# A ninth weight unit beside the ring, a first gather that also turns, a later weight vector, and the last expert's sums kept in the banks

## The chip, the cores and the metric

The kernel runs on one core of one Trainium2 chip. The time is that of the device in microseconds (us), from the program's start to its end; the median of several executions counts. All engines work side by side: TensorE (PE) multiplies, VectorE (DVE) and ScalarE (ACT) do elementwise work, GpSimd (POOL) helps a little, and SyncE (SP) issues nearly all transfers (DMA).

## What is computed

One layer of a decoder on 336 token rows (272 of a prompt with its 16 meta tokens, 64 of samples): a mixing part (RWKV-7 heads and a convolution), then a mixture of 32 experts of which each token takes 4, then a last RMS norm. The change touches the expert part and the last norm. Cut to those, the reference is:

```python
h2 = rms_norm(x, norm_ffn)
logits = h2 @ w_router + b_router
top_val, top_idx = lax.top_k(logits, TOP_K)          # 4 of 32
gates = jax.nn.softmax(top_val, axis=-1)
# for every expert e, on the tokens that chose it:
gt = jnp.minimum(xe @ w_gate[e] + b_gate[e], SWIGLU_LIMIT)
up = jnp.clip(xe @ w_up[e] + b_up[e], -SWIGLU_LIMIT, SWIGLU_LIMIT)
ye = ((up + 1.0) * gt * jax.nn.sigmoid(SWIGLU_ALPHA * gt)) @ w_down[e] + b_down[e]
x = x + (sum over the token's experts of gates * ye)
y = rms_norm(x, norm_final)
```

All weights are float32, 1024 x 1024 each: 12.6 MB per expert, 402.7 MB for the 32 experts.

## The kernel before

**Stages.** The first 245 us hold the mixing part. Then the router scores all tokens, and the loop over the 32 experts runs, four experts to a turn: expert 0 to 3 are written out ahead of the loop, 28 to 31 behind it. Each expert works on one block of 64 token slots.

**One expert on PE** (`body`). `gate_up` multiplies the block xT with w_gate (bank 0) and w_up (bank 1), eight chunks of 128 rows each, and adds the bias with two small bf16 products. Then `combine` of the expert before: six products that spread its rows ys back to the tokens, into six banks (`CMB_BANKS = [5, 4, 3, 2, 6, 7]`). Then `next_rows` gathers the next expert's rows from h by a one-hot matrix Pm (bank 5), `turn_act` transposes the activation, `turn_p` transposes the combining matrix, `turn` transposes the gathered rows, and `down` multiplies with w_down (bank 2). DVE clamps and multiplies (`glu`), adds the six banks to the running sum acc (`add_rows`), and makes the one-hot matrices and xT (`take_x`); ACT computes the sigmoid and copies banks out (`take_rows`, `take_act`, `take_down`).

**Weight units.** A weight matrix comes in two units of 2 MB (128 partitions x 16 KB), so an expert has six: k = 0 and 1 gate, 2 and 3 up, 4 and 5 down, 6 is the next expert's first, and so on. They lie in a ring of NSLOT = 8 slots, unit k in slot k % 8. PE counts `unit_used` up by one when it is through with a unit. SP issues the units in order, all in one queue: the first eight once their places are free of the stages before (`FREED_BY`), and unit k from 8 on when `unit_used` says that unit k - 8 has been used, in the code's words `UPRE + k - NSLOT + 1`, which is k - 7 uses in the expert part. PE waits for a unit's own semaphore (`landed`). The last unit of all comes in two halves.

**Ahead of expert 0** (lines 1828 to 1845 and the code ahead of the bodies). When `p_ready` says that DVE has made the one-hot matrix Pm0, PE gathers the block's rows from acc (L1834, 12 matmul records, bank 5), ACT copies them to xg (L1631), PE transposes them (L1841, bank 5), DVE multiplies by the norm weights into xT (`take_x(1)`, L2064), and the first gate product begins (L1856). Between them stand `idle_product`s, products of nothing that is used (L1813). A record here is one matmul instruction as the trace has it; a float32 product takes two of them.

**Rows h.** ACT writes h, the scaled rows for the gathers of experts 1 to 31, over words 0 to 3071 of the arena, which x2T, the turned input, held before.

**Behind expert 31.** `combine` of the last expert (L1910); `add_tile` on DVE adds the six banks to acc (L2199); ACT squares and sums each tile's rows (`norm`, L1685) and takes the root (`root`, L1691); DVE takes the reciprocal (L2204) and multiplies rows, reciprocal and gfin, the final norm's weights (L2205); SP stores the outputs. There are three tiles of tokens: 128, 128 and 80 rows. gfin, 512 KB (one row laid out over 128 partitions), is fetched by SP right ahead of the first weight unit (L1502).

## Time and profile before

| | us |
|---|---|
| median of 3 runs | 1222.55 |
| lowest and highest | 1222.38, 1223.22 |
| the profiled execution, whole | 1223.54 |
| its span, from the first instruction to the last | 1221.6 |

| engine | busy, share of the span |
|---|---|
| PE matmul | 97% |
| PE weight load | 44% |
| DVE | 37% |
| ACT | 16% |
| POOL | 3% |
| transfers, mean of 16 DMA engines | 85% |

A page of the profile has a line per engine over 40 equal slices of the span (30.5 us each), a digit for the busy tenths, and the bytes moved per slice. Below that one can ask for the chain of work that ended last, for the instructions in order of time, and for the busy time of each engine in stretches of one's own choice. PE's busy time is that of pipelined matmuls whose ends overlap the next one's start, so several records in a row are read as (end of the last - start of the first - length of one) / (number - 1), which is called the pitch below.

### The profile page before, as it was taken

What the parts mean: (1) busy time and instruction counts of PE and PEld (TensorE: products, weight loads), DVE (VectorE), ACT (ScalarE), POOL (GpSimd) and SP (SyncE); (2) the same over time, 40 slices, a digit from 0 to 9 for tenths busy, and PEclk for the clock granted to TensorE, in tenths of its full rate; (3) what the DMA queues carried; (4) which work ended last, traced back from release to release, by engine and by line L of the source; (5) the groups of instructions that cost most, each with busy time, mean ns of one, the idle gap of its engine ahead of it and who ended that gap; (6) DMA issues with size and microseconds to landing.
All of it is one profiled execution on the core that took longest, in us unless ns stands there. A gap on an engine that the chain in (4) does not pass through costs nothing.

```text
span 1221.6 us, 19136 instructions
## 1 busy us (share of the span) xinstructions
PE 1187.9 (97%) x8044; PEld 535.9 (44%) x8044; DVE 453.2 (37%) x993; ACT 199.4 (16%) x437; POOL 30.8 (3%) x34
## 2 busy tenths in 40 slices
PE   8999999999999999999999999999999999999995
PEld 6676799764333333333333333333333333333332
DVE  6899442253533322222322333322222222222224
ACT  3345323123101000100100001100010000001002
POOL 0000050030000000000000000000000000000000
PEclk9999999999999999999999999999999999999998
DMA  9524000398999999999999999999999999999994
GB/s 261 178 69 184 11 4 13 90 383 329 429 425 424 428 426 428 428 429 428 428 429 428 427 429 429 428 428 429 428 429 428 427 428 429 428 429 428 427 428 155
DMA packets 53596, 430.25 MB, mean 352 GB/s; under 512 B 12175, under 2 KB 25919, under 8 KB 28702
## 3 DMA queue, kind: packets, MB, share of 16 engines
q1 hardware_dynamic: 53314, 428.91, 85.1%
q8 instruction: 43, 0.70, 0.2%
q10 hardware_dynamic: 228, 0.55, 0.1%
q14 instruction: 11, 0.09, 0.0%
HBM read 424.92 MB, written 4.48 MB: 352 GB/s over the span
## 4 chain that ended last, share of the span: by engine, by line
PE 66%; DMA 19%; DVE 1%; ACT 1%; issue 0%; POOL 0%; DVEq 0%
PE bank L1856 41%; DMA ring<-in_w_up_dram 19%; PE bank L1834 6%; PE bank L1910 5%; PE bank L1096 3%; PE bank L1841 2%; PE bank L1181 2%; PE bank L1785 2%; PE bank L1461 1%; PE bank L1864 1%; PE bank L1051 1%; PE bank L1077 1%; PE bank L1882 1%; PE bank L1234 0%; PE bank L1230 0%; PE bank L1139 0%
## 5 line engine op out<-in xcount | busy, mean ns | idle before, releaser
L1856 PE MATMUL bank<-ring,arena 128*64 128x512 f32 x1536 | 342.2, 594 | 7.5 <-DMA ring<-in_w_up_dram 6.8
L1856 PE MATMUL bank<-arena 128*64 128x512 f32 x1536 | 342.5, 593 | 6.1 <-DMA arena<-in_w_up_dram 6.0
L1856 PEld LDWEIGHTS bank<-ring,arena 128*64 128x64 f32 x1536 | 109.1, 137 | 218.9 <-issue 200.6
L1856 PEld LDWEIGHTS bank<-arena 128*64 128x64 f32 x1536 | 108.9, 136 | 216.9 <-issue 199.4
L2131 DVE TENSOR_SCALAR arena<-bank 128x512 f32<-128x512 f32 x32 | 22.1, 692 | 380.2 <-PE bank L1864 380.2
L2145 DVE TENSOR_TENSOR arena<-arena,bank 128x512 f32<-128x512 f32 x186 | 113.7, 679 | 1.6 <-PE bank L1910 1.6
L540 PE MATMUL bank<-arena,ring 128*128 128x336 f32 x352 | 102.8, 447 | 0.3 <-ACT arena L357 0.3
L1910 PE MATMUL bank<-arena 64*128 64x512 f32 (+1 forms) x384 | 91.1, 606 | 0.7 <-issue 0.7
L1834 PE MATMUL bank<-arena 128*64 128x512 f32 (+1 forms) x384 | 89.5, 600 | 0.1
L2135 DVE TENSOR_SCALAR arena<-bank 128x512 f32<-128x512 f32 x32 | 22.1, 692 | 176.4 <-PE bank L1864 176.4
L540 PEld LDWEIGHTS bank<-arena,ring 128*128 128x128 f32 x352 | 65.8, 189 | 33.9 <-issue 2.5
L1631 ACT COPY arena<-bank 128x512 f32<-128x512 f32 x32 | 18.8, 587 | 368.0 <-PE bank L1834 368.0
L762 DVE SCALAR_TENSOR_TENSOR arena<-ring,arena 128x336 f32<-128x336 f32 x120 | 58.5, 562 | 0.0
L1644 ACT ACTIVATE arena<-arena 128x512 f32<-128x512 f32 x32 | 20.2, 631 | 227.7 <-DVE arena L2131 227.7
L1910 PEld LDWEIGHTS bank<-arena 64*128 64x128 f32 (+1 forms) x384 | 31.9, 172 | 52.7 <-issue 52.7
L1654 ACT COPY arena<-bank 128x512 f32<-128x512 f32 x32 | 18.8, 586 | 221.5 <-PE bank L1856 221.5
L1834 PEld LDWEIGHTS bank<-arena 128*64 128x64 f32 (+1 forms) x384 | 24.9, 136 | 61.9 <-issue 56.1
L1841 PEld LDWEIGHTS bank<-arena 128*128 128x128 f32 x256 | 35.8, 210 | 26.8 <-DVE arena L2145 25.2
L2087 DVE TENSOR_SCALAR arena<-arena 128x128 f32<-128x128 f32 (+1 forms) x96 | 27.5, 342 | 49.9 <-PE bank L1882 49.7
L1841 PE MATMUL bank<-arena 128*128 128x128 f32 x256 | 45.8, 301 | 0.0
L2133 DVE TENSOR_TENSOR arena<-arena 128x512 f32<-128x512 f32 x32 | 22.2, 693 | 22.3 <-ACT arena L1644 22.3
L1864 PE MATMUL bank<-arena 96*64 96x512 bf16 x128 | 24.9, 381 | 0.0
(359 smaller groups left out, 784.6 us busy)
## 6 DMA issues: line engine op xcount, KB each, us to landing
ring<-in_w_gate_dram SPq DMA_DIRECT2D x32, 2048.0 KB, 24.5
arena<-in_w_up_dram SPq DMA_DIRECT2D x32, 2048.0 KB, 27.6
ring<-in_w_down_dram SPq DMA_DIRECT2D x32, 2048.0 KB, 31.0
arena<-in_w_gate_dram SPq DMA_DIRECT2D x32, 2048.0 KB, 26.3
ring<-in_w_up_dram SPq DMA_DIRECT2D x32, 2048.0 KB, 28.8
arena<-in_w_down_dram SPq DMA_DIRECT2D x31, 2048.0 KB, 30.7
ring<-in_w_in_dram SPq DMA_DIRECT2D x11, 1024.0 KB, 7.9
ring<-in_w_out_dram SPq DMA_DIRECT2D x4, 1024.0 KB, 8.1
```

What stands on the lines that cost most here:

```text
L540: mm = M.matmul(bank[:, n % 4, 0:NT], w[:, c, b * P:b * P + P], hT[:, c, :], start=(c == 0), stop=(c == KC - 1))
L762: V.scalar_tensor_tensor(dst, src, w, dst, ALU.mult, ALU.add).then_inc(R["conv_step"], 1)
L1096: mm = M.matmul(dst[64 * i:64 * i + n, q, j, 0:n], lhs[64 * i:64 * i + n, q, j, 0:n], rhs[64 * i:64 * i + n, q, j, 0:n], start=True, stop= ...
L1181: mm = M.matmul(bank1(b)[64 * i:64 * i + n_out, j, 0:n_free], lhs(i, j), rhs(i, j), start=(first and j == 0), stop=(last and j == NPAIR - 1))
L1785: mm = M.matmul(bank[:, (d + 1) % 4, 0:NT], out_rows(cc)[:, P * d:P * d + P], yT[:, cc, :], start=(cc == 0), stop=(cc == 3))
L1834: mm = M.matmul(bank[64 * hb:64 * hb + 64, 5, :], sel[0:m, i, :], rows[0:m, i, 512 * hb:512 * hb + 512], start=(i == 0), stop=(i == 2))
L1841: mm = M.transpose(bank[:, b, m * P:m * P + P], src.rearrange("t (p q) -> t q p", q=4)[:, m, :], ident)
L1856: mm = M.matmul(bank[64 * hb:64 * hb + 64, b, :], tokens(cc), w[:, c, 512 * hb:512 * hb + 512], start=(cc == 0), stop=(w3 == 2 and cc == K ...
L1864: mm = M.matmul(bank[64 * hb:64 * hb + 64, b, :], esel[0:3 * NE, :], bias2[0:3 * NE, w3, 512 * hb:512 * hb + 512], start=False, stop=True)
L1910: M.matmul(bank[0:m, bk, :], PgT[64 * hb:64 * hb + 64, i, 0:m], ys[64 * hb:64 * hb + 64, :], start=not biased, stop=True).then_inc(F["cmb_ ...
L2087: last = V.tensor_scalar(Pg[0:m, i], b2(slot_iota[0:m, :], 2), col(i, m), gates[0:m, i, bass.ds(e, 1)], ALU.is_equal, ALU.mult)
L2145: V.tensor_tensor(o, o, bank[0:m, CMB_BANKS[k], :], ALU.add).then_inc(F["cmb_read"], 1)
```

## The change

**Second unit outside the ring.** Unit 1 is no longer in the ring. It is fetched in two halves of 1 MB into `second`: words 29824 to 31871 and 0 to 2047 of the arena, which is free once x2T has been transposed for the last time (`acc_turned` 6). Units 0, 2, 3, ... 8 take the eight slots (`place(k, shift=1)`: unit k in slot (k - 1) % 8 from then on). Unit 9 goes in when unit 0 has been used; unit k from 10 on waits for k - 7 uses, as before. Since h overlies the second half, ACT writes h only when two units have been used.

**First gather turned at once.** Gather, copy, transposition and the three idle products ahead of expert 0 go. In their place PE makes xT in two banks: 24 products whose stationary operand is a strided part of acc (every fourth column, 128 of them) and whose moving operand is Pm0 with 64 columns. Bank 5 gets the first half (`x0_done`), bank 4 the second (`x_done`). DVE scales each half by itself. The first gate unit waits for the first half alone, the second for both.

**gfin last.** The transfer of the final norm's weights is issued behind the last weight unit.

**Last expert's sums in the banks.** For expert 31, `combine` of expert 30 moves between its gate and its up product, and `add_rows` on DVE with it. A new function `seed` writes the running sum acc into a bank, by a product with the identity matrix. Seeds 0, 4 and 5 stand ahead of `turn_act` of expert 31, seeds 1 and 2 behind its down product, seed 3 behind the wait for ys; the last `combine` adds on top of them. DVE's six additions behind it go. ACT squares straight from the two banks of a tile, and DVE multiplies straight from the banks, in two instructions of 512 columns per tile, once all six are done. The table load for the root moves ahead of the last copy of ys. `over_blocks`, which handles experts with more than 64 tokens, gets a hook that writes the banks back to acc; with these inputs it does not run.

The diff, cut to its core:

```diff
+        second = [at_word(29824, 2, DM), at_word(0, 2, DM)]
+        def place(k, shift=1):
+            return (k - shift) % NSLOT
 # SP
-                sp.dma_start(gfin, a["norm_final"].rearrange("(o d) -> o d", o=1).broadcast_to([P, DM])).then_inc(F["gfin_in"], 16)
-                for k in range(NSLOT):
-                    if FREED_BY[k]:
-                        sp.wait_ge(unit_used, FREED_BY[k])
-                    start_unit(sp, k // EU, k)
+                for s in range(NSLOT):
+                    k = s + 1 if s else 0
+                    if s == 7:
+                        sp.wait_ge(F["acc_turned"], 6)
+                        for half in range(2):
+                            sp.dma_start(second[half], unit_src(0, 1)[:, 2 * half:2 * half + 2, :])\
+                                .then_inc(extra_landed, 16)
...
+                    if FREED_BY[s]:
+                        sp.wait_ge(unit_used, FREED_BY[s])
+                    start_unit(sp, k // EU, k, s)
-                for k in range(NSLOT, PER):
-                    sp.wait_ge(unit_used, UPRE + k - NSLOT + 1)
-                    start_unit(sp, k // EU, k)
+                for k in range(NSLOT + 1, PER):
+                    sp.wait_ge(unit_used, UPRE + (k - NSLOT + 1 if k > NSLOT + 1 else 1))
+                    start_unit(sp, k // EU, k, place(k))
...
+                sp.dma_start(gfin, a["norm_final"].rearrange("(o d) -> o d", o=1).broadcast_to([P, DM])).then_inc(F["gfin_in"], 16)   # behind the last unit
 # ACT
-                take_rows(1)
+                act.wait_ge(unit_used, UPRE + 2)      # ahead of writing h
+                    if last:
+                        A.activation(small[:, 50:51], eps_fin, ACT.Sqrt)
                     take_down(at)
-                    act.wait_ge(F["cmb_read"], 6 * (NE - 1) + 2 * i + 2)
-                    norm(i)
+                    act.wait_ge(F["cmb_done"], 6 * (NE - 1) + 2 * i + 2)
+                    norm(i, bank[0:TILES[i][1], b:b + 2, :])
 # PE
+                def seed(k):
+                    M.matmul(bank[0:m, CMB_BANKS[k], :], ident[0:m, 0:m], acc[0:m, i, 512 * hb:512 * hb + 512],
+                             start=True, stop=False)
-                gather(acc, Pm0)
-                idle_product(1)
-                pe.wait_ge(F["xg_ready"], 1)
-                turn(xg, 5).then_inc(F["x_done"], 1)
-                idle_product(2)
+                for u in range(2):
+                    for q in range(4):
+                        for i, (t0, m) in enumerate(TILES):
+                            mm = M.matmul(bank[:, 5 - u, P * q + C * u:P * q + C * u + C],
+                                          acc[0:m, i, 512 * u:512 * u + 512].rearrange("t (p q) -> t q p", q=4)[:, q, :],
+                                          Pm0[0:m, i, :], start=(i == 0), stop=(i == 2))
+                    mm.then_inc(F["x_done"] if u else F["x0_done"], 1)
...
+                    gate_up(at, over, first, earlier_rows if last else None)
...
+                    if last:
+                        pe.wait_ge(F["cmb_read"], before(6, 6))
+                        for k in (0, 4, 5):
+                            seed(k)
...
-                pe.wait_ge(F["cmb_read"], 6 * (NE - 1))
-                combine(counter(NE - 1))
+                seed(1)
+                pe.wait_ge(F["pgt_ready"], NE)
+                seed(2)
+                combine(counter(NE - 1), seeded=True)     # seed(3), then the six products
 # DVE
-                add_tile(0)
-                add_tile(1)
-                scale(0, 1)
-                add_tile(2)
-                scale(1, 2)
-                scale(2, 3)
+                dve.wait_ge(F["cmb_done"], last_at(6, 6))
+                for i in range(3):
+                    scale(i, i + 1, in_bank)              # two instructions of 512 columns each
```

**The order on PE ahead of expert 0.** The rows are PE's products in order, with the number of calls (a call is two records, a transposition one). Before:

```order
L1825 MATMUL bank<-arena 128x32 x3
L1813 MATMUL bank<-arena 64x512 x2
L1834 MATMUL bank<-arena 64x512 x6
L1813 MATMUL bank<-arena 64x512
L1841 MATMUL bank<-arena 128x128 x4
L1813 MATMUL bank<-arena 64x512 x2
L1856 MATMUL bank<-ring,arena 64x512 x16
```

And of the changed kernel, the same place:

```order
L1841 MATMUL bank<-arena 128x32 x3
L1829 MATMUL bank<-arena 64x512 x2
L2012 MATMUL bank<-arena 128x64 x24
L1881 MATMUL bank<-ring,arena 64x512 x8
L1881 MATMUL bank<-arena 64x512 x8
L1889 MATMUL bank<-arena 64x512 x2
```

Gather, transposition and three idle products have become 24 products with 64 moving columns, and the gate product of 16 calls now reads its second half from outside the ring.

**The order on PE in expert 31 and behind it.** Before, from the end of its up product:

```order
L1864 MATMUL bank<-arena 64x512 x2
L1910 MATMUL bank<-arena 128x512 x4
L1910 MATMUL bank<-arena 80x512 x2
L1841 MATMUL bank<-arena 128x128 x4
L1882 MATMUL bank<-arena 128x128 x2
L1882 MATMUL bank<-arena 128x80
L1856 MATMUL bank<-ring,arena 64x512 x8
L1856 MATMUL bank<-arena 64x512 x8
L1910 MATMUL bank<-arena 128x512 x4
L1910 MATMUL bank<-arena 80x512 x2
```

And of the changed kernel, from the end of its gate product (L1881 is a weight product, L1889 its bias, L1947 combine, L1928 seed, L1857 and L1907 the transpositions):

```order
L1947 MATMUL bank<-arena 128x512 x4
L1947 MATMUL bank<-arena 80x512 x2
L1881 MATMUL bank<-arena 64x512 x16
L1889 MATMUL bank<-arena 64x512 x2
L1928 MATMUL bank<-arena 128x512
L1928 MATMUL bank<-arena 80x512 x2
L1857 MATMUL bank<-arena 128x128 x4
L1907 MATMUL bank<-arena 128x128 x2
L1907 MATMUL bank<-arena 128x80
L1881 MATMUL bank<-ring,arena 64x512 x16
L1928 MATMUL bank<-arena 128x512 x3
L1947 MATMUL bank<-arena 128x512 x4
```

The six products of combine of expert 30 now stand ahead of the up product; three seeds follow the up product, three more the down product.

## Rows read from the trace of the kernel before

**Rows 1.** The page's 40 slices: GB/s moved.

```profile
GB/s 261 178 69 184 11 4 13 90 383 329 429 425 424 428 426 428 428 429 428 428 429 428 427 429 429 428 428 429 428 429 428 427 428 429 428 429 428 427 428 155
```

**Rows 2.** The chain that ended last: start us, length us, what.

```profile
340.49 13.89 PE bank L1856 x64
...
368.69 13.89 PE bank L1856 x64
...
805.87 32.97 DMA ring<-in_w_up_dram
```

**Rows 3.** Stretches: length, busy us by engine, granted clock, DMA share, GB/s.

```profile
292.00:294.00 2.00, 2.00 (x12) 0.75 (x10) 1.72 (x8) 2.00 (x3) 0.00 (x0) 1.00 0.06 21
294.00:296.00 2.00, 2.00 (x12) 0.86 (x10) 0.00 (x0) 1.64 (x2) 0.00 (x0) 1.00 0.00 0
296.00:298.00 2.00, 2.00 (x12) 0.80 (x10) 0.00 (x0) 0.00 (x0) 0.00 (x0) 1.00 0.97 262
...
345.00:346.00 1.00, 1.00 (x6) 0.29 (x4) 0.00 (x0) 0.00 (x0) 0.00 (x0) 1.00 0.91 344
```

**Rows 4.** Transfers issued by SP: start us, length of the issuing, what.

```profile
295.11 3.78 SPq L1442 DMA_DIRECT2D ring<-in_w_up_dram  x2
...
314.00 0.33 SPq L1442 DMA_DIRECT2D arena<-in_w_gate_dram  x1
...
344.11 3.76 SPq L1442 DMA_DIRECT2D arena<-in_w_gate_dram  x2
```

**Rows 5.** Ahead of expert 0, in order of time: start us, length us, engine, line.

```profile
286.16 2.80 PE L1834 MATMUL bank<-arena 128*64 128x512 f32 x12
...
289.74 0.56 PEld L1841 LDWEIGHTS bank<-arena 128*128 128x128 f32 x4 [0.81 <-ACT arena L1631]
...
290.63 0.69 DVE L2064 TENSOR_TENSOR arena<-bank,arena 128x512 f32<-128x512 f32 x1 [4.33 <-PE bank L1841]
...
291.43 7.09 PE L1856 MATMUL bank<-ring,arena 128*64 128x512 f32 x32
```

**Rows 6.** Weight loads of 128 columns that lie side by side, ahead of short products.

```profile
280.33 0.66 PEld L1800 LDWEIGHTS bank<-arena 128*128 128x128 f32 x6 [0.71 <-ACT arena L1612]
...
281.46 1.32 PEld L1772 LDWEIGHTS bank<-arena 128*128 128x128 f32 x12
```

**Rows 7.** PE in expert 31, in order of time.

```profile
1187.72 3.61 PE L1856 MATMUL bank<-arena 128*64 128x512 f32 x16
1192.29 3.65 PE L1856 MATMUL bank<-ring,arena 128*64 128x512 f32 x16 [0.96 <-DMA ring<-in_w_up_dram]
...
1196.09 2.85 PE L1910 MATMUL bank<-arena 64*128 64x512 f32 x12
1198.92 0.72 PE L1841 MATMUL bank<-arena 128*128 128x128 f32 x4
...
1200.36 3.65 PE L1856 MATMUL bank<-ring,arena 128*64 128x512 f32 x16 [0.38 <-DVE arena L2145]
```

**Rows 8.** A product with 128 stationary and 512 moving columns, PE, an early stage.

```profile
51.44 2.74 PE L565 MATMUL bank<-arena 65*128 65x512 f32 x6
```

**Rows 9.** The chain that ended last, behind expert 31's down product.

```profile
1207.45 0.72 issue
1208.17 1.15 PE bank L1910 x4
...
1210.70 1.16 ACT ring L1685 x2
...
1211.88 0.30 ACT arena L1691
...
1216.62 1.28 DVE arena L2205
```

**Rows 10.** DVE in expert 31: one from a bank, one from the arena.

```profile
1196.20 0.69 DVE L2135 TENSOR_SCALAR arena<-bank 128x512 f32<-128x512 f32 x1 [6.19 <-PE bank L1864]
1196.93 0.69 DVE L2137 SCALAR_TENSOR_TENSOR arena<-arena 128x512 f32<-128x512 f32 x1
```

More of the change, by code:

```diff
@@ L1915, in body, with earlier_rows @@
                     before = counter(it, GROUP, r - 1)
-                    over = (r, it * (16 * PER // NSLOT))
-                    gate_up(at, over)
-                    if not first:
+                    over = (r, it * (16 * PER // NSLOT), 1)
+                    def earlier_rows():
                         if not second:
@@ L2158, in body @@
                         make_p(rank_next)
-                    glu(at, at(1, 1))
-                    if not first:
-                        add_rows(counter(it, GROUP, r - 1))
+                    earlier = counter(it, GROUP, r - 1)
+                    glu(at, at(1, 1), (lambda: add_rows(earlier)) if last else None)
+                    if not first and not last:
+                        add_rows(earlier)
                     if not last:
@@ L2192, in _, with scale @@
                 last_at = counter(NE - 1)
[L2194 to L2201 removed]
+                def scale(i, k, rows):
                     n = TILES[i][1]
```

138 lines of the change are left out of this document (85 added, 53 removed).

## The prediction

> **What bounds the kernel now.** First the 40 slices of the page [rows 1]. The transfers move 425 to 429 GB/s in every slice from the eleventh to the last but one; in the fifth to eighth they rest, and the ninth and tenth fall short. So from about 305 us on the memory never pauses. Next the chain of waits [rows 2]. It runs over PE for the first experts, at 368.69 - 340.49 = 28.20 us each, and only from 805.87 us on do transfers stand in it. An expert's weights are six units of 2.10 MB, and at 428 GB/s a unit takes 4.90 us, an expert 29.4. PE is thus 1.2 us per expert faster than the memory and eats up a lead until about 806 us. The end is set by the transfers: their last unbroken start, plus the remaining bytes, plus what PE, DVE and ACT do behind the last units. A gain must move that start or shorten that tail.
>
> Where does the unbroken stretch begin? The stretches [rows 3] show a hole: 21 GB/s from 292 to 294 us, nothing from 294 to 296. All eight slots were full and no unit was used. At 295.11 SP issues unit 8 [rows 4], when PE has used unit 0; the first bytes come about 1 us later, and the first 2 us run at 262 instead of 428 GB/s, a loss of 0.33 MB or 0.8 us. From 296 us ten units (8 to 17) need 296 + 0.8 + 10 x 4.90 = 345.8 us. Unit 18 waits for the eleventh use, and is issued at 344.11 [rows 4], ready to flow at 345.1. So it comes only about 0.7 us before the queue is empty, and the stretch from 345 to 346 in fact falls to 344 GB/s and a share of 0.91 [rows 3]: some of the 16 engines did run dry. This is the point on which the first half of the change turns: **the ring's releases, that is PE's pace, pin the stream at unit 18**, not the hole at 292.
>
> **The ninth unit and gfin.** Both fill or empty the queue ahead of the hole: one unit more is 4.9 us more to move, gfin's 0.52 MB leaving is 1.2 us less. The bytes of the first fill would end some 3.7 us later than at about 291, at 294.8. Yet unit k from 10 on still waits for k - 7 uses. With PE later by d (below), unit 9 is issued at 295.1 + d, unit 10 two uses or 7 us after that, and unit 12 at 314.0 + d [rows 4]. With d = 0.7: unit 9 flows from 296.8 to 302.5, units 10 and 11 from 303.7 to about 314.3, unit 12 from 315.7. Two holes of over 1 us and a rest of the first have taken the place of the old one, and the extra unit is spent. Then six units from 315.7 + 0.8 give 345.9, and unit 18, issued at 344.8, is ready at 345.8. Fetching gfin last costs nothing: it is 1.2 us behind the last unit, and is needed some 10 us after that. Its cover is the down product; without it the last scaling would wait 1.2 us.
>
> The extra unit itself is issued behind `acc_turned` 6. PE's last loads for the turned rows end at 281.46 + 1.32 = 282.8 us [rows 6], and the queue then holds one whole unit, so it lands at about 291. The first gate product needs it 3.5 us after its start, at 295.6. Behind this wait SP has queued unit 8 and b_down, neither due yet.
>
> ACT's three instructions for h now wait for two uses, about 299 us, and behind them stand the table load and the first sigmoid. DVE needs that sigmoid only ahead of `u_done`, at about 306; 3.2 us of h, a load of 1.3 and 0.6 of sigmoid end near 304. That is hidden by the up product, at no cost.
>
> **The first gather.** Before, from PE's start at 286.16 to the first gate product at 291.43 it takes 5.27 us [rows 5]: gather, copy, transposition, DVE. Now it is 24 calls or 48 records, each with its own load of 128 stationary columns. The trace has no such product with strided columns and 64 moving ones. Its bounds: loads of columns side by side go at 0.66 / 6 = 0.11 us and 1.32 / 12 = 0.11 [rows 6], whatever moves; the transposition that loads every fourth column goes at 0.56 / 4 = 0.14 [rows 5], which still holds the tail of its last one. So 48 records are 5.3 to 6.7 us. I take 0.125, as that row's tail must come off: 6.0 us, gate product at 292.2, **d = 0.7** later (0.0 to 1.4). DVE's first half is hidden by PE's second; its second half is due 3.5 us into the gate product. The ACT copy and the handovers that go are not saved, since PE's own work is as long as the whole old chain. The three idle products lay in those waits and return nothing.
>
> The Trainium skill, page "TensorE: Matmul & The Clock Gate", section "LDWEIGHTS (loading the stationary operand)", puts the load at columns / 1.2 ns, 107 ns for 128, whatever the rows, and has no price for a stride. The rows with columns side by side agree (0.11); by it d would be -0.1, the stream 0.6 us earlier instead of 0.4 later, and the time 1222.9.
>
> **What d does to the end.** Unit 18 is issued d later; 0.7 us of slack was there, but 16 engines that run dry begin again with up to 0.8 us of loss. I take the stream **0.4 us later** at the end (from -0.6, with d = 0, where unit 12 starts at 315.0 and the ten units end 0.6 earlier, to 1.5).
>
> **Expert 31.** The up product started at 1187.72 as its unit landed, and PE stood 0.96 us ahead of its second unit at 1192.29 [rows 7]. Six products of combine now stand ahead of it: 2.85 us with the last one's tail, 2.7 without. Up then starts at 1190.4 and its second unit, 3.5 us later, at 1193.9: **1.6 us later** than before, of 2.7 inserted. Then combine's old place (1196.09, now 1197.7) is held by three seeds, six records. The nearest row has 128 stationary and 512 moving columns: 2.74 / 6 = 0.46 at most, 0.43 without the tail [rows 8], so 2.6 us. DVE's two steps for the activation end at 1199.2, so PE is the later one: `turn_act` at 1200.3. From there to the down product it took 1200.36 - 1198.92 = 1.44 us [rows 7], now until 1201.75: **1.4 us later** than 1200.36. The last unit lands at 1192.3 + 2 x 4.9 = 1202.1 and its half is not needed before 1207, so the down product does not wait. Before, DVE's additions covered this place; they now lie beside the up product.
>
> **Behind it.** Call the end of the down product E (before, 1207.45). Before, combine began at E + 0.72 and the last scaling ended at 1216.62 + 1.28 = 1217.90, E + 10.45 [rows 9]. Now three seeds, 2.6 us, begin 0.2 ahead of E and cover the copy of ys: combine at E + 2.4. All six products are done 2.85 later, E + 5.25. ACT's norms start at E + 3.6 and take 1.46 each (1.16 + 0.30), so the last root is ready at E + 8.0. DVE then does three tiles of a reciprocal, 0.2, and two multiplications from banks. One from a bank and one from the arena both show 0.69 [rows 10], and 1.33 for the two overlapped is the nearest to 1.28 for one of 1024. That is 1.55 a tile, E + 5.3 + 4.65 = E + 9.95: **0.5 us less**, from +0.5 (seeds at 0.46, DVE's six at 0.69 each without overlap) to -0.7. Stores follow as before.
>
> The same skill, page "VectorE: DVE Perf Modes", section "The TRN2 errata — SBUF-src ops pay a fixed extra latency per instruction", gives a source in PSUM 120 cycles of fixed cost instead of 58, 0.065 us more. Rows 10 show no difference; by it these six instructions would be 0.4 us more, and the time 1224.3.
>
> **The sum.** The stream +0.4, expert 31 +1.4, the end -0.5: +1.3 us. The profiled execution's span is 1221.6 and would be 1222.9. That execution took 1223.54 in all, 1.0 above the median, so the change is laid on the median: 1222.55 + 1.3 = **1223.9 us**. A measurement of this kernel can tell about 0.2%, 2.4 us, from no change.
>
> **The rivals.** *The lead is kept* (0.08): if transfers were not pinned at unit 18, filling the hole would give a whole unit. For it speaks the hole itself, against it the order of releases and the dip at 345. 1222.55 - 4.9 + 0.9 = 1218.6. *Short products run at the pace of their moving columns* (0.06): 64 columns of 512 that take 0.43 would be 0.055, 48 of them 2.6 us; all releases come 2.6 earlier, and here the ninth unit would be of use. 1222.55 - 2.6 + 0.9 = 1220.9. The loads in rows 6, with 32 moving columns at 0.11, speak against it. *Slower, by the strided load* (0.11): if a full product's load, read at every fourth column, overlaps less than the transposition's, at 0.185, 48 records take 8.9 us, d is 3.6, the stream 3.4 later: 1226.9. It decides from about 0.15 a record on, where the sum passes 2.4 us. *The extra unit is late* (0.03): if it lands behind 295.6, each microsecond is one of PE and of the end. Something that I do not see, either way: 0.04. The forecast as worked out, with its bounds, 0.68.
>
> **The numbers.** The forecast's own bounds add up to -0.6 + 1.4 - 0.7 and 1.5 + 1.4 + 0.5: 1222.6 to 1226.0. The range takes in the second rival as well: 1220.8 to 1226.0, with 0.07 of the forecast's chance above 1225.0, the edge of 0.2%. Faster by over 0.2% is the first rival and half of the unseen, 0.08 + 0.02 = 0.10; slower is the third, most of the fourth, the other half of the unseen and that upper end, together 0.22; within, 0.68.
>
> **What would show it.** The first gate product starts at 292.2 (right), before 291 (second rival) or after 294 (third). Holes in GB/s near 295, 303 and 315 and none behind 346: right; an unbroken stream from 246: first rival. The transfers' first place in the chain stays near 806. Expert 31's down product starts 1.4 us later against its last landing up unit, and the last scaling ends 10 us behind that product. It would be wrong if the end of the stream moved by over 1.5 us.

## The result, and the profile after

The changed kernel takes **1232.6 us** (median of four runs, 1232.0 to 1233.2) against 1222.7 for the kernel before on the same chip (four runs, 1222.4 to 1223.2): 1.0077 times as long, 95% interval 1.0066 to 1.0089, or 9.9 us. The forecast was 1223.9 us in a range of 1220.8 to 1226.0. It is outside, and on the side of the third rival, the strided load, but beyond its price too.

The profiled execution took 1232.0 us with a span of 1230.2, against a span of 1221.6: 8.6 us more in the two traces. The profiled execution of before (1223.54) is above all the timed ones, that of after is the shortest of its four, which is where the rest up to 9.9 lies. The working below goes by the traces.

First the slices of the page, as in [rows 1]:

```profile
GB/s 252 185 69 183 11 4 13 100 390 277 371 419 426 427 429 426 427 428 430 428 427 428 430 428 428 429 429 427 429 429 428 427 430 429 427 427 430 426 427 162
```

The tenth slice has 277 GB/s where [rows 1] has 329, and the eleventh (from 307.6 us) 371 where it has 429. From the thirteenth on nothing differs by more than a few GB/s. Whatever costs 8.6 us has happened by about 370 us, or behind the last weights.

PE around the first gather, in order of time (start us, length us, engine, line and tiles):

```profile
286.19 11.46 PE L2012 MATMUL bank<-arena 128*128 128x64 f32 x48
297.59 5.53 PE L1881 MATMUL bank<-ring,arena 128*64 128x512 f32 x16
302.95 3.60 PE L1881 MATMUL bank<-arena 128*64 128x512 f32 x16
```

These rows answer to [rows 5]. PE starts on the gather at 286.19, as before (286.16). The 48 records (L2012) take 11.46 us, 0.44 of it the length of one: the pitch is 11.02 / 47 = 0.235 us (0.233 from one weight load to the next), not 0.125. The gate product starts at 297.59, not at 291.43 as before or 292.2 as forecast. And its first unit takes until 302.95, 5.36 us, where the 32 records of L1856 in [rows 5] took 7.09, or 3.5 for the same 16.

The stretches show why that first unit is slow too (columns: length; busy us and instructions of PE, PE's weight loads, DVE, ACT, POOL; granted clock; DMA share; GB/s):

```profile
286.00:288.00 2.00, 1.87 (x10) 1.81 (x8) 0.34 (x4) 0.42 (x2) 0.00 (x0) 0.94 0.78 295
288.00:290.00 2.00, 2.00 (x11) 2.00 (x10) 0.00 (x0) 0.00 (x0) 0.00 (x0) 0.50 0.98 406
...
296.00:298.00 2.00, 2.00 (x10) 1.77 (x11) 0.30 (x1) 0.00 (x0) 0.00 (x0) 0.50 0.68 183
298.00:300.00 2.00, 2.00 (x6) 0.48 (x4) 1.90 (x14) 0.00 (x0) 0.00 (x0) 0.50 0.04 13
300.00:302.00 2.00, 2.00 (x8) 0.62 (x6) 0.50 (x4) 0.00 (x0) 0.00 (x0) 0.65 0.00 0
302.00:304.00 2.00, 2.00 (x12) 0.70 (x10) 0.00 (x0) 0.00 (x0) 0.00 (x0) 1.00 0.00 0
```

Before, the granted clock was 1.00 in this place [rows 3]. Now it is 0.50, the lower of TensorE's two levels (1.2 instead of 2.4 GHz), from within the row of short products until about 301.4 us, by when the gate product has run for 3.8 us: 6 records in the stretch from 298 to 300, where 12 go at the full clock. That costs 5.36 - 3.5 = 1.9 us more. In the last column one sees what follows: the transfers rest from 298 to 304, six microseconds, where the forecast had holes of one.

SP's transfers, next to [rows 4] (the columns as there):

```profile
303.16 0.35 SPq L1448 DMA_DIRECT2D ring<-in_w_up_dram  x1
...
322.04 3.76 SPq L1448 DMA_DIRECT2D arena<-in_w_gate_dram  x2
...
352.14 0.33 SPq L1448 DMA_DIRECT2D ring<-in_w_gate_dram  x1
```

These rows begin with units 9, 12 and 18 (a row of two begins with the first). Unit 12 is issued 8.0 us later than the 314.00 of [rows 4], and unit 18 8.0 later than 344.11. That is the lateness of the first use: 6.2 at the gate's start and 1.9 in its first unit. The last weights land at 1209.18 us, read from the list of transfers, against 1201.64 before: **7.5 later**, 0.5 less than the 8.0.

PE in expert 31 and behind it, next to [rows 7]:

```profile
1195.04 2.85 PE L1947 MATMUL bank<-arena 64*128 64x512 f32 x12
1197.81 7.09 PE L1881 MATMUL bank<-arena 128*64 128x512 f32 x32
...
1205.05 2.85 PE L1928 MATMUL bank<-arena 128*128 128x512 f32 x6
1207.74 0.63 PE L1857 MATMUL bank<-arena 128*128 128x128 f32 x4
...
1209.09 7.09 PE L1881 MATMUL bank<-ring,arena 128*64 128x512 f32 x32 [0.43 <-issue]
1216.11 2.85 PE L1928 MATMUL bank<-arena 128*128 128x512 f32 x6
1218.89 2.85 PE L1947 MATMUL bank<-arena 64*128 64x512 f32 x12
```

The up product now runs through without its wait of 0.96 us, the seeds (L1928) take 2.7 us to the start of the transposition, and the down product begins at 1209.09, 8.7 later than 1200.36, thus **1.2 us** more than the last landing is late. The last landing wanders by itself, though. PE's waits are the steadier mark. Its last wait in expert 30, before and after:

```profile
1162.92 3.66 PE L1856 MATMUL bank<-arena 128*64 128x512 f32 x16 [1.24 <-DMA arena<-in_w_up_dram]
```

```profile
1170.13 3.65 PE L1881 MATMUL bank<-ring,arena 128*64 128x512 f32 x16 [1.07 <-DMA ring<-in_w_up_dram]
```

From there to the down product it takes 37.44 us before and 38.96 after, and in between the changed kernel waits for no unit any more: **1.5 us** later, with the stream 7.2 later. The sum is the same 8.7. DVE's last instructions, next to [rows 9]:

```profile
1221.87 0.16 DVE L2255 RECIPROCAL arena<-arena 128x1 f32<-128x1 f32 x1 [15.29 <-PE bank L1947]
1222.07 1.41 DVE L2257 SCALAR_TENSOR_TENSOR arena<-bank,arena 128x512 f32<-128x512 f32 x2
...
1225.10 1.40 DVE L2257 SCALAR_TENSOR_TENSOR arena<-bank,arena 80x512 f32<-80x512 f32 x2
```

With E = 1209.09 + 7.09 = 1216.18 the last scaling ends at 1226.50, E + 10.3, against E + 10.45 before: **0.1 less**. The three together, 7.5 + 1.2 - 0.1, are the 8.6 us of the spans (7.2 + 1.5 - 0.1 by the other mark).

### The profile page after: what moved, and what is told of

It reads as the page before. It is cut to its first block, busy times and chain, and to the rows that moved or that the text cites. A ratio compares the mean times of both kernels' runs of the same rounds, so it can differ in the third digit from the quotient of the medians.

```text
span 1230.2 us, 19213 instructions
## 1 busy us (share of the span) xinstructions
PE 1199.1 (97%) x8082; PEld 545.0 (44%) x8082; DVE 449.7 (37%) x991; ACT 198.6 (16%) x436; POOL 30.7 (2%) x34
## 4 chain that ended last, share of the span: by engine, by line
PE 70%; DMA 17%; DVE 1%; ACT 0%; issue 0%; POOL 0%; DVEq 0%
PE bank L1881 43%; DMA arena<-in_w_up_dram 8%; DMA ring<-in_w_up_dram 8%; PE bank L1947 6%; PE bank L1850 6%; PE bank L1857 2%; PE bank L1096 2%; PE bank L1181 2%; PE bank L1801 1%; PE bank L1467 1%; PE bank L2012 1%; PE bank L1889 1%; PE bank L1051 1%; PE bank L1077 1%; PE bank L1907 1%; PE bank L1928 0%
## 5 line engine op out<-in xcount | busy, mean ns | idle before, releaser
L1881 PE MATMUL bank<-ring,arena 128*64 128x512 f32 x1536 | 344.0, 596 | 6.2 <-DMA ring<-in_w_up_dram 5.7
L1881 PE MATMUL bank<-arena 128*64 128x512 f32 x1536 | 342.4, 593 | 6.5 <-DMA arena<-in_w_up_dram 6.5
L1881 PEld LDWEIGHTS bank<-ring,arena 128*64 128x64 f32 x1536 | 109.5, 137 | 217.5 <-issue 201.2
L1881 PEld LDWEIGHTS bank<-arena 128*64 128x64 f32 x1536 | 107.5, 136 | 219.0 <-issue 202.5
L1947 PE MATMUL bank<-arena 64*128 64x512 f32 (+1 forms) x384 | 91.1, 606 | 0.0
L1850 PE MATMUL bank<-arena 128*64 128x512 f32 x372 | 86.7, 600 | 0.0
L1947 PEld LDWEIGHTS bank<-arena 64*128 64x128 f32 (+1 forms) x384 | 31.7, 172 | 52.0 <-issue 52.0
L1850 PEld LDWEIGHTS bank<-arena 128*64 128x64 f32 x372 | 23.9, 135 | 60.0 <-issue 55.1
L1857 PEld LDWEIGHTS bank<-arena 128*128 128x128 f32 x252 | 35.3, 210 | 25.7 <-DVE arena L2202 24.3
L1857 PE MATMUL bank<-arena 128*128 128x128 f32 x252 | 45.0, 301 | 0.0
L1889 PE MATMUL bank<-arena 96*64 96x512 bf16 x128 | 24.8, 381 | 0.0
```

The source lines that it names most:

```text
L1850: mm = M.matmul(bank[64 * hb:64 * hb + 64, 5, :], sel[0:m, i, :], rows[0:m, i, 512 * hb:512 * hb + 512], start=(i == 0), stop=(i == 2))
L1857: mm = M.transpose(bank[:, b, m * P:m * P + P], src.rearrange("t (p q) -> t q p", q=4)[:, m, :], ident)
L1881: mm = M.matmul(bank[64 * hb:64 * hb + 64, b, :], tokens(cc), w[:, 512 * hb:512 * hb + 512], start=(cc == 0), stop=(w3 == 2 and cc == KC - 1))
L1889: mm = M.matmul(bank[64 * hb:64 * hb + 64, b, :], esel[0:3 * NE, :], bias2[0:3 * NE, w3, 512 * hb:512 * hb + 512], start=False, stop=True)
L1947: M.matmul(bank[0:m, bk, :], PgT[64 * hb:64 * hb + 64, i, 0:m], ys[64 * hb:64 * hb + 64, :], start=not (biased or seeded), stop=True).then ...
```

## The experiments

The theory after reading the trace: nearly all the loss is the strided stationary operand of the 24 products, with the fall of the clock in its wake, handed on at full length by unit 18's release. The rivals: the ninth unit or the order of the transfers; the handling of the last expert; a clock that falls first and makes the products slow. Times are medians beside runs of the kernel before on the same chip, ratios come with a 95% interval.

### The old first gather in the changed kernel

The changed kernel with `gather`, copy and `turn` ahead of expert 0 as before:

```diff
-                for u in range(2):
-                    for q in range(4):
-                        for i, (t0, m) in enumerate(TILES):
-                            mm = M.matmul(...)            # the 24 products
+                gather(acc, Pm0)
+                idle_product(1)
+                pe.wait_ge(F["xg_ready"], 1)
+                turn(xg, 5).then_inc(F["x_done"], 1)
+                idle_product(2)
```

> The changed kernel with gather, copy, transposition and idle products ahead of expert 0 as in the kernel before; ninth unit, gfin last and the banks for the last expert stay. Theory S (the 24 products with strided stationary columns cost all of the loss in the head): the first gate product starts at about 291.4 us again, TensorE's granted clock stays at 1.0 there, the time is before -0.3 for the head and +1.1 for the tail, so 0.5 to 1.5 us above before. Rival U (the ninth unit or its late landing costs part): over 2 us above before. Rival L (the filled hole in the transfers is kept): about 3.8 us below before.

1225.2 us against 1223.4, ratio 1.0010 (1.0001 to 1.0019). 8 of the 10 us are gone with this one part. Unit 18 is issued at 344.21, as before. What stays, 1.2 us by the ratio and 1.8 by the medians, is to be looked for at the end. In its profile the last weights land 2.0 us later than before (1203.68), but PE's wait in expert 30 ends only 0.6 later (1163.49), and from there to the down product it takes 38.96 us as in the changed kernel: 0.6 + 1.5 - 0.1 is its span's 2.0.

### The ninth unit and gfin alone

The same, and expert 31 and the end as before too.

```diff
-                        if last:
-                            pe.wait_ge(F["cmb_read"], before(6, 6))
-                            for k in (0, 4, 5):
-                                seed(k)
...
-                    gate_up(at, over, first, earlier_rows if last else None)
+                    gate_up(at, over, first)
```

> The kernel before with only the ninth unit outside the ring and gfin fetched last. Theory P (the ring's releases pin the stream at unit 18): 0 to 0.6 us below before, with a new hole in the transfers near 303 and 314 us in place of the one near 294. Rival L (the lead is kept): 4.9 us below before. Rival U (the extra unit lands late, or h written later delays the sigmoid): slower by over 1 us.

1224.1 us, ratio 1.0002 (0.9993 to 1.0011): nothing that shows, and not the 4.9 us of a lead that is kept. The stretches of this kernel, as in [rows 3]:

```profile
294.00:296.00 2.00, 2.00 (x12) 0.75 (x10) 0.90 (x5) 0.00 (x0) 0.00 (x0) 1.00 0.97 418
303.00:305.00 2.00, 2.00 (x12) 0.85 (x10) 0.04 (x1) 1.91 (x2) 0.00 (x0) 1.00 1.01 332
314.00:316.00 2.00, 2.00 (x12) 0.71 (x10) 1.81 (x9) 0.00 (x0) 0.00 (x0) 1.00 0.48 201
345.00:347.00 2.00, 2.00 (x12) 0.71 (x10) 0.00 (x0) 0.00 (x0) 0.00 (x0) 1.00 0.94 311
```

The hole at 294 is filled (418 GB/s, where [rows 3] has 0), and in its place come a dip at 303 (332 GB/s) and a hole at 315 (201), behind the same uses of the units. The queue still runs low at 345. Before, the last weights landed 1201.64 - 344.11 = 857.5 us after the issue of unit 18; here 1202.71 - 345.26 = 857.5. So the stream counts from there, whatever lay ahead.

### Expert 31 and the end alone

Changed: the order in expert 31, the seeds, and the scalings from the banks; first gather, units and gfin as before.

```diff
+                    if last:
+                        pe.wait_ge(F["cmb_read"], before(6, 6))
+                        for k in (0, 4, 5):
+                            seed(k)
...
-                scale(2, 3)
+                for i in range(3):
+                    scale(i, i + 1, in_bank)
```

> The kernel before with only the change to expert 31 and what follows it (combine ahead of the up product, seeds, sums kept in the banks). From the two traces: the down product of expert 31 starts 1.2 us later against the last landing up unit, and the end behind it is 0.1 us shorter, so 1.1 us above before. Rival: what the traces show as 1.2 belongs to the head's shift, and the part by itself is even or gains 0.5.

1224.3 us, ratio 1.0009 (1.0000 to 1.0018), a loss of 1.1 us. From the last weights to the span's end it is 1221.70 - 1200.38 = 21.3 us, before 1221.60 - 1201.64 = 20.0. From PE's wait in expert 30 it is 1221.70 - 1161.63 = 60.1, before 1221.60 - 1162.92 = 58.7. So this part costs 1.1 to 1.4 (the interval of the ratio goes from 0 to 2.2), which is what the first experiment left over.

### The first gather alone

The kernel before with nothing but the 24 products (and one wait of ACT for acc ahead of writing h, which the old gather implied).

```diff
-                gather(acc, Pm0)
-                idle_product(1)
-                pe.wait_ge(F["xg_ready"], 1)
-                turn(xg, 5).then_inc(F["x_done"], 1)
-                idle_product(2)
+                for u in range(2):
+                    for q in range(4):
+                        for i, (t0, m) in enumerate(TILES):
+                            mm = M.matmul(...)            # the 24 products
```

> The kernel before with only the 24 products in place of gather, copy and transposition (plus one wait on acc that keeps it free of a race). Theory S: 48 records at 0.233 us, 11.2 us instead of 5.3, then about 2 us for a gate unit at the lower clock: the stream and the end 7 to 8 us later, time 7 to 8.5 us above before. Rival: without the ninth unit the stream is pinned differently and the loss is under 6 or over 9 us.

1232.0 us, ratio 1.0072 (1.0056 to 1.0087): the loss of the whole change. PE's row of the products, and three stretches of it, in this kernel:

```profile
286.39 11.46 PE L1994 MATMUL bank<-arena 128*128 128x64 f32 x48
```

```profile
288.00:290.00 2.00, 2.00 (x11) 2.00 (x10) 0.00 (x0) 1.98 (x3) 0.00 (x0) 1.00 0.96 406
290.00:292.00 2.00, 2.00 (x10) 2.00 (x10) 0.00 (x0) 1.04 (x1) 0.00 (x0) 0.65 0.80 268
294.00:296.00 2.00, 2.00 (x10) 2.00 (x10) 0.00 (x0) 0.00 (x0) 0.00 (x0) 0.50 0.00 0
```

In this execution the clock fell only at 290.6. The first four microseconds thus ran at the full clock, and just as slowly: 10 loads in 2 us at 1.00, 10 at 0.65, 10 at 0.50. The fall of the clock doesn't make these products slow. It comes in their wake, and its price is paid by the dense product behind them. The stretch without any transfer (0 GB/s at 294) also shows that other traffic isn't the cause, since it has 10 loads like the one with 406.

### The same products with the stationary columns side by side

The changed kernel; only which 128 columns of acc a product loads. (Expert 0's channels then come in another order than its weights, so its result is not the reference's.)

```diff
-  acc[0:m, i, 512 * u:512 * u + 512].rearrange("t (p q) -> t q p", q=4)[:, q, :]
+  acc[0:m, i, 512 * u:512 * u + 512].rearrange("t (q p) -> t q p", q=4)[:, q, :]
```

> The changed kernel, but the 24 products load 128 stationary columns of acc that lie side by side instead of every fourth; this takes the channels in another order than the weights have them, so expert 0's result is not the reference's, and nothing else differs. Theory S (the stride sets the pace): 48 records at 0.11 us, 5.3 us, the first gate product at about 291.5, time 1 to 1.5 us above before, the same as with the first gather as before. Rival M (a short moving operand costs 0.23 whatever the stationary's layout): 11 us as with the stride, time 9 to 10 above before. On the clock: if it falls whenever 48 such short products run, it falls here too and the gate unit takes 5 us instead of 3.4.

1224.1 us, ratio 1.0004 (0.9994 to 1.0014). PE, in order of time, and a stretch:

```profile
285.87 5.57 PE L2012 MATMUL bank<-arena 128*128 128x64 f32 x48
291.37 3.65 PE L1881 MATMUL bank<-ring,arena 128*64 128x512 f32 x16
```

```profile
288.00:290.00 2.00, 2.00 (x20) 2.00 (x20) 0.42 (x1) 0.00 (x0) 0.00 (x0) 1.00 1.00 418
```

The 48 records take 5.57 us, 0.28 of it the length of one, so 5.29 / 47 = 0.113 us of pitch (0.111 from load to load, as in [rows 6]); 20 loads in 2 us instead of 10. The clock stays at 1.00 and the gate product's first unit takes 3.5 us. Stride alone turns 5.5 us into 11.4.

### Twice the moving columns

The changed kernel with each moving operand of 64 columns written twice into 128, the stationary one strided as in the change.

```diff
-                            mm = M.matmul(bank[:, 5 - u, P * q + C * u:P * q + C * u + C], ...
-                                          Pm0[0:m, i, :], ...
+                            mm = M.matmul(bank[:, 5 - u, P * q:P * q + P], ...
+                                          Pm0[0:m, i, :].unsqueeze(1).broadcast_to([m, 2, C]), ...
```

> The changed kernel, with the moving operand of the 24 products written twice (128 columns instead of 64, the second copy lands in columns that nobody reads). Theory S: the load paces, so a record still takes 0.23 us and the stretch 11.2 to 11.5 us. On the clock: if the fall to half comes from too few moving columns in the stretch, twice as many may keep it at full speed, the first gate unit takes 3.4 instead of 5.4 us and the time is 2 us below the changed kernel's, 7.5 to 8 above before; if the strided load or the length of the stretch brings it, the clock falls all the same and the time stays 9 to 10 above before.

1230.4 us, ratio 1.0063 (1.0046 to 1.0080). PE's row of the products, and the stretches of this kernel:

```profile
287.58 11.47 PE L2012 MATMUL bank<-arena 128*128 128x128 f32 x48
```

```profile
290.00:292.00 2.00, 2.00 (x10) 2.00 (x10) 0.00 (x0) 0.00 (x0) 0.00 (x0) 0.70 0.96 401
292.00:294.00 2.00, 2.00 (x10) 2.00 (x10) 0.31 (x1) 0.00 (x0) 0.00 (x0) 0.50 1.13 479
294.00:296.00 2.00, 2.00 (x11) 2.00 (x10) 0.11 (x1) 0.00 (x0) 0.00 (x0) 0.95 0.99 426
```

Twice the columns cost nothing (11.47 against 11.46 us), so the price is the load's. The clock was low for 3.4 us only and back before the gate product, whose first unit took 3.4 us. The time is 7.1 us above before where the changed kernel's is 9.9. That would be about the 1.9 of the slow first unit, but there are three executions and the two intervals overlap. Why the clock was low for so much shorter isn't shown: with 64 columns it was low for 13.65 us in one profile and for 10.24 in another, and this is a single profile too.

### The strides, one by one

Which strides cost? The kernel before, with seven rows of products of nothing that is used ahead of expert 1's gate product, 12 calls each.

```diff
+                    if second:
+                        pe.wait_ge(F["x_ready"], at(1, 1))
+                        for c in range(12):      # so with q = 1, 2, 4 and 8
+                            M.matmul(bank[:, 0, 0:C], h[:, 0, 0:128 * q].rearrange("t (p q) -> t q p", q=q)[:, c % q, :],
+                                     ident[:, 0:C], start=True, stop=True)
+                        for c in range(12):      # so with q = 1 and 4, then the first row again
+                            M.transpose(bank[:, 0, 0:P], h[:, 0, 0:128 * q].rearrange("t (p q) -> t q p", q=q)[:, c % q, :], ident)
```

> The kernel before, with seven rows of products of nothing that is used ahead of expert 1's gate product, 12 calls each: products with 128 stationary columns of h side by side, then every second, fourth and eighth column, 64 moving columns each; then transpositions of 128 columns side by side and of every fourth; then side by side again. It measures the disputed price by itself. Theory, from the first gather (0.233 us per record with every fourth column, 0.111 side by side, and 0.14 for the transposition that reads every fourth): every stride above one doubles a full float32 product's load, so 24 records take 2.7 us side by side and 5.6 with every second, fourth or eighth column, and a transposition takes 0.11 to 0.14 either way. Rival: the price grows with the stride (0.15 to 0.17 at every second column, 0.23 at every fourth, more at every eighth), since it is bytes passed over. Second rival: the doubling belongs to the place and not to the stride (the ninth unit and the matrices that DVE makes read and write the same memory beside it), then all rows here are at 0.11. The time is longer by what the rows add to PE ahead of unit 18, some 23 us by the theory, and says nothing else.

PE in order of time. In this order: side by side, every second, every fourth, every eighth column, transpositions side by side and of every fourth, side by side again.

```profile
316.83 2.89 PE L1920 MATMUL bank<-arena 128*128 128x64 f32 x24
319.56 3.01 PE L1923 MATMUL bank<-arena 128*128 128x64 f32 x24
322.41 5.81 PE L1926 MATMUL bank<-arena 128*128 128x64 f32 x24
328.01 5.92 PE L1929 MATMUL bank<-arena 128*128 128x64 f32 x24
333.73 2.77 PE L1932 MATMUL bank<-arena 128*128 128x128 f32 x12
336.29 2.59 PE L1934 MATMUL bank<-arena 128*128 128x128 f32 x12
338.71 2.79 PE L1936 MATMUL bank<-arena 128*128 128x64 f32 x24
```

From start to start, by 24 records: 0.114, **0.119**, **0.233**, 0.238. So neither my theory (every stride doubles) nor the first rival (more with each) holds: every second column is as good as free, every fourth doubles, and every eighth adds nothing to that. The second rival, that the place and the traffic do it, falls: the price is the same in another stage, from another tile. The row of every fourth column began at the full clock (322.4 to 324.9) and went on at half; it has the pitch of the first gather all the same.

The two rows of transpositions take 2.56 and 2.42 us from start to start, and inside both a record follows the last one after 0.213 us. They ran at half the clock (0.50 from 324.9 to 338.6 in this execution), and so are no test of the stride: by [rows 8] 512 moving columns take 0.43 us at the full clock, so 128 take about 0.11 there and 0.21 at half (an estimate), and a load's price below that would not show. The trace of the kernel before has the test, at the full clock. L1841 transposes every fourth column, L1882 columns side by side (number of records, then ns of one: least, median, most):

```profile
L1841 PEld LDWEIGHTS bank<-arena x256: 195/212/221, 289.7 to 1199.2; 128*128 128x128 f32 x128
L1882 PEld LDWEIGHTS bank<-arena x96: 138/139/157, 308.8 to 1199.6; 128*128 128x128 f32 x64, 80*128 80x128 f32 x32
```

The load with the stride is longer in a transposition too, 0.21 against 0.14 us. But from load to load it is 0.12 against 0.11 (four from 308.33 to 308.80, three from there to 309.14). So with the stride a transposition takes **about a tenth longer** and a product **twice as long**; the product's load records are 0.33 us at every fourth column (L1926) against 0.19 (L1920).

The time of this one execution, 1246.9 us, only says that PE's insert of 24.6 us ahead of unit 18 comes out at the end nearly whole: its span is 23.5 us longer.

### A delay ahead of unit 18, and one behind it

Is it PE's lateness at unit 18 that counts, and nothing else? Twelve products of nothing that is used (5.1 us to the gate product behind them) in the kernel before: once ahead of expert 1's gate product, once ahead of expert 3's.

```diff
+                    if second:                    # the other kernel: r == 3, outside the loop
+                        pe.wait_ge(F["x_ready"], at(1, 1))
+                        for hb in range(12):
+                            M.matmul(bank[64 * (hb % 2):64 * (hb % 2) + 64, 0, :], ones[:, 0:C], h[:, 0, 0:512],
+                                     start=True, stop=True)
```

> The kernel before with 12 idle products (5.1 us of TensorE) ahead of expert 1's gate product. Theory P (releases pin the stream at unit 18, whose margin is 0.7 us at most): unit 18 is issued 5.1 us later, the stream and the end 4.4 to 5.2 us later. Rival (eight units of lead absorb a delay of TensorE, since the end is set by the transfers alone): within 0.5 us of before.

> The kernel before with the same 12 idle products ahead of expert 3's gate product instead. In the trace of before, unit 30 (released by the first down unit of expert 3) is issued at 400.66 and its first byte moves at 404.85, so 1 us after issue it has about 3.2 us of margin: theory P gives 5.1 - 3.2 = 1.9 us above before, up to 2.7 with the loss at a restart. Rival (all absorbed): within 0.5. Rival (nothing absorbed, TensorE itself is the bound): 5.1.

Expert 1: 1227.6 us against 1223.3, ratio 1.0038 (1.0023 to 1.0052), 4.3 us for 5.1. Expert 3: 1224.8, ratio 1.0015 (1.0006 to 1.0025), 1.5 us for the same 5.1. Stretches of the first, then of the second:

```profile
350.00:352.00 2.00, 2.00 (x12) 0.71 (x10) 0.00 (x0) 0.00 (x0) 0.00 (x0) 1.00 0.08 33
```

```profile
344.00:346.00 2.00, 2.00 (x12) 0.72 (x10) 0.00 (x0) 0.00 (x0) 0.00 (x0) 1.00 1.08 442
...
406.00:407.00 1.00, 1.00 (x8) 0.34 (x6) 0.00 (x0) 0.00 (x0) 0.00 (x0) 1.00 0.27 82
```

The first opens a hole of 2 us where before there was a dip. Unit 18's issue, and PE's last wait for a unit, in the first:

```profile
351.92 3.76 SPq L1442 DMA_DIRECT2D arena<-in_w_gate_dram  x2
```

```profile
1200.09 3.65 PE L1856 MATMUL bank<-ring,arena 128*64 128x512 f32 x16 [0.96 <-DMA ring<-in_w_up_dram]
```

From the one to the other it is 848.2 us. Before it was 1192.29 - 344.11 = 848.2 too, with the ninth unit alone 848.1 and with the first gather alone 848.0. **So a delay of unit 18's release comes out at the end one for one.**

The second kernel leaves 345 untouched and has a short hole at 406, where unit 30 is issued (406.02 instead of 400.66). There the margin is larger by what PE gains in two experts, 2 x 1.2 us: 0.7 + 2.4 = 3.1, and 5.1 - 3.1 = 2.0 is near the 1.5 measured. The pin is confirmed, its margin of 0.7 is not: in these profiles 0 to 0.2 us of the delay is absorbed (in the changed kernel 0.5 to 0.8 of its 8.0, and why more isn't shown). The medians' 4.3 for 5.1 would fit 5.1 - 0.7 = 4.4, but its interval is 2.8 to 6.4. (In the profiled execution of the first, the stages ahead were 2.7 us late as well, so its rows stand at later times than its median would.)

### Unit 18 released earlier

If releases pin the stream, then earlier ones should help, until something else pins it. b_down, a product that gives the `combine` in expert 1's body the bias of w_down, moves from there to the one in expert 3's body, so unit 18 comes 1.8 us sooner. Once in the kernel before, once with ninth unit and gfin last.

```diff
-                        combine(before, biased=second)
+                        combine(before, biased=biased)
...
-                    body(0, r, first=(r == 0), second=(r == 1))
+                    body(0, r, first=(r == 0), second=(r == 1), biased=(r == 3))
```

> The kernel before with the product of the gates and b_down (six calls, 1.9 us of TensorE) added in the combine of expert 2 instead of expert 0, so that it stands behind unit 18's release. Theory P: unit 18 is issued 1.9 us earlier; the stream then runs unbroken from 296 us on and is bound by its own bytes, so it gains what engines running dry at unit 18 lost, 0.2 to 0.8 us, and the time is 0 to 0.8 below before. Rival (the releases play no part): no change at all, and the dip at 345 us stays.

> The same move of the b_down product, together with the ninth unit and gfin last; first gather and end as in the kernel before. Theory P: with unit 18 out of the way unit 12 is the pin (issued at 314.0, margin 1.4 us), so the stream gains 0.6 to 1.4 us against before and the time is 0.5 to 1.5 below it. Rival L (the ninth unit's 4.9 us come through once unit 18 is free): 4 to 5 below.

1222.4 us, ratio 0.9996 (0.9986 to 1.0006), and 1222.2, ratio 0.9994 (0.9985 to 1.0003). SP's issue of unit 18 in the first (unit 12 and 18 in the second):

```profile
342.30 3.76 SPq L1442 DMA_DIRECT2D arena<-in_w_gate_dram  x2
```

```profile
314.16 3.76 SPq L1448 DMA_DIRECT2D arena<-in_w_gate_dram  x2
...
342.35 0.33 SPq L1448 DMA_DIRECT2D ring<-in_w_gate_dram  x1
```

Both release unit 18 1.8 us earlier, and neither gains what a measurement can tell. In the first the old hole at 294 would take over: ten units from 296.8 end at 345.8, and the last weights land at 1201.56 instead of 1201.64. In the second that hole is filled, but unit 12 comes at 314.16 behind a hole (176 GB/s from 314 to 316), and the six units behind it end at nearly the same time; the last weights land at 1201.24, 0.4 earlier. By this working three places lie within one microsecond of each other, so none of them alone is worth what could be measured. That fits the forecast's picture of the ninth unit; that just these holes are the next pins is worked out, not tested by itself. Neither version beats the kernel before by more than its interval.

## Why the prediction was wrong, and where it was right

**The step that failed: the price of the first gather.** The prediction took 0.125 us per record, from bounds of 0.11 (loads side by side) and 0.14 (the transposition of every fourth column, [rows 5]). It is 0.233 to 0.235. The transposition was chosen as the nearest row since it has the same stride. It is a different instruction for this purpose: with the stride its loads follow each other after 0.12 instead of 0.11 us, while a full float32 product's take 0.233 instead of 0.111. The upper bound was thus no bound. The trace of before had a sign of it, which the forecast didn't read: the transposition's load records are 0.21 us long with the stride and 0.14 without. The third rival had the right mechanism (0.185 a record), and its price of 3.6 us for d was still too small. The gate product was 6.2 us later than before instead of 0.7.

**A step that was not there: the clock.** The forecast let PE run at the full clock throughout [rows 3]. It fell to half within the row of strided products at 0.233 us, and the first gate unit took 1.9 us more. The three idle products that go were counted as free, as they were in time. Whether they would have kept the clock up behind such a row wasn't tried; side by side, without them, it stayed up.

**What d does to the end: right.** The prediction let all of d but 0.2 to 0.3 us reach the end (0.4 of 0.7, 3.4 of 3.6); 8.0 us at unit 18 gave 7.5 by the last landing. With the right d its own working would have said about 1231: by the third rival's step (3.4 us for a d of 3.6) the stream is 7.9 later, and 1222.55 + 7.9 + 0.9 = 1231.3. These 8.8 us agree with the 8.6 of the spans; the 9.9 of the medians are a microsecond more, which no run explains.

**The ninth unit and gfin: right.** Nothing measurable by itself (1.0002), a dip near 303 and a hole near 315 in place of that at 294, a low queue at 345. ACT's later h was hidden, and gfin landed before it was needed, at 1210.4 against a first use at 1222.1.

**Expert 31: right.** 1.2 us by the last landing, 1.5 by PE's wait in expert 30, against a forecast of 1.4. **Behind it: right in kind, off in size.** 0.1 us less instead of 0.5. The seeds are the term: combine began at E + 2.7 instead of E + 2.4, as six seed records take 2.78 us where 2.6 was taken, and begin 0.07 ahead of E instead of 0.2. DVE's part, 4.65 forecast, took 4.63. Both together cost 1.0 in the trace, or 1.4 by PE's wait; 0.9 was forecast, and 1.1 measured alone.

**The chain** has its first transfer at 841.71, not near 806 as in [rows 2]:

```profile
827.77 13.91 PE bank L1881 x64
841.71 33.55 DMA arena<-in_w_up_dram
```

That is an expert later than 805.87 + 8.0. PE gains only 1.2 us per expert on the memory, so a few tenths decide in which expert the chain first meets the transfers; with the first gather alone it is 813.73. That changes nothing at the end.

## What to carry to other kernels

Before a product takes a strided stationary operand in float32, have its price per record measured: every fourth column doubled it here, every second was nearly free (0.119 us against 0.114), and a transposition with the same stride took 0.12 us against 0.11, so gather and turn in two steps was the faster way. A bound must come from the same kind of instruction, not from one that shares only the access pattern. And in a stream that a ring's releases pin, first find all places with nearly the same margin: filling one hole moves nothing while the next is a microsecond behind, but each microsecond lost ahead of the pin counts nearly in full.

## What the runs showed of the hardware

- The load of 128 stationary columns for a float32 product follows the one before it after 0.111 to 0.114 us per record side by side, 0.119 at every second column, 0.233 to 0.235 at every fourth and 0.238 at every eighth, at the full clock and at half of it alike (10 loads in 2 us at 1.00 and at 0.50, with every fourth column). 64 or 128 moving columns make no difference at every fourth column.
- A transposition of 128 columns takes 0.213 us at half the clock, side by side and at every fourth column alike. At the full clock its loads follow each other after 0.11 us side by side and 0.12 at every fourth column (their records last 0.14 and 0.21).
- In the profiled executions the granted clock fell to 0.50 within 1.6 us of the first strided record (changed kernel), 4.2 (gather alone) and 2.5 (the strides), and stayed there for 13.65, 10.24 and 13.65 us. With 128 moving columns it fell after 3.2 us and was back after 3.41. At 0.111 us per record and 64 moving columns it didn't fall. Each is a single profile.
- Two of DVE's multiplications of 512 columns from a bank, one behind the other, took 1.41 us, so 0.7 each, next to the 0.69 from the arena in [rows 10]: no extra price of the bank shows.
